# Attention scores of both mixers in steps of two heads of each key head, and no masked key tile for query tile 0

## What is computed

```python
# first mixer: window_attention, query blocks of 128, keys |i - j| <= 128 of 256, and 256 context keys
logits = concat([q . k (valid), q . k_ctx]) * HEAD_DIM ** -0.5
p = softmax(concat([logits, sink_of_head]))[..., :-1]
out = p @ concat([v, v_ctx])

# second mixer: nsa_attention, for each query block of 128
p_cmp = softmax(where(cmp_ok, q . k_cmp, NEG_INF)) * cmp_ok
p_slc = softmax(where(key_pos <= t_idx, q . k_sel, NEG_INF))
p_win = softmax(where(kpos <= t_idx, q . k_win, NEG_INF))
o = g0 * (p_cmp @ v_cmp) + g1 * (p_slc @ v_sel) + g2 * (p_win @ v_win)
```

## Time and profile before

| | us |
|---|---|
| median of 3 runs | 2797.01 |
| lowest and highest of them | 2795.85, 2802.97 |
| the profiled execution | 2805.34 |
| span in its profile | 2803.4 |
| PE busy | 2281.8 (81%) |
| DVE busy | 1179.1 (42%) |
| ACT busy | 497.4 (18%) |
| POOL busy | 1080.0 (39%) |

### The profile page before, as it was taken

One profiled execution on the slowest core, in us unless ns is written; L12 is line 12 of the kernel. 1 busy time (PEld: TensorE's weight loads), 2 busy tenths in 40 slices (PEclk: granted clock), 3 DMA queues, 4 the chain that ended last, 5 costly groups with the idle time before them and its releaser, 6 DMA issues.

```text
span 2803.4 us, 21791 instructions
## 1 busy us (share of the span) xinstructions
PE 2281.8 (81%) x7703; PEld 1058.7 (38%) x7703; DVE 1179.1 (42%) x2839; ACT 497.4 (18%) x1068; POOL 1080.0 (39%) x1028
## 2 busy tenths in 40 slices
PE   6998877787777776977788777779886789998997
PEld 2463832222222225722222222234454353443433
DVE  1241666665656445766656755420344230101001
ACT  2131121121112111211112111110133110000001
POOL 0000377777677660777777777700000000000000
PEclk9968999999999998999999999989856889999998
DMA  8424499999999992899999999944500079999996
GB/s 329 150 90 156 180 391 409 409 406 407 406 407 406 404 398 93 306 408 409 407 407 406 384 376 391 409 166 144 177 0 1 9 283 395 395 393 393 393 394 238
DMA packets 292277, 864.10 MB, mean 308 GB/s; under 512 B 19372, under 2 KB 26668, under 8 KB 291912
## 3 DMA queue, kind: packets, MB, share of 16 engines
q0 software_dynamic: 147456, 536.94, 48.7%
q1 hardware_dynamic: 144712, 325.74, 31.2%
HBM read 861.55 MB, written 1.05 MB: 308 GB/s over the span
## 4 chain that ended last, share of the span: by engine, by line
PE 37%; DMA 29%; POOL 17%; issue 7%; DVE 5%; ACT 4%; SPq 2%; POOLq 0%; DVEq 0%; ACTq 0%
PE bank L1604 18%; DMA ring<-in_up,arena 15%; DMA arena<-in_w_up 9%; POOL arena L631 8%; POOL ring L631 8%; PE bank L1809 5%; PE bank L2061 5%; DMA arena<-in_up,arena 4%; SPq L603 2%; PE bank L1646 2%; PE bank L1658 1%; PE bank L1659 1%; PE bank L2104 1%; PE bank L1713 1%; ACT h L653 1%
## 5 line engine op out<-in xcount | busy, mean ns | idle before, releaser
L1809 PE MATMUL bank<-arena 128*128 128x512 f32 x1024 | 516.9, 639 | 147.3 <-DMA arena<-in_up,arena 112.4
L1809 PE MATMUL bank<-ring,arena 128*128 128x512 f32 x976 | 496.2, 636 | 161.8 <-DMA ring<-in_up,arena 161.6
L1151 DVE SCALAR_TENSOR_TENSOR ring<-ring,h 128x1024 f32<-128x1024 f32 x256 | 313.1, 1225 | 324.8 <-DMA ring<-in_down,arena 324.4
L631 POOL DMA_INDIRECT arena<-in_down,arena x256 | 264.7, 1034 | 478.2 <-DVE arena L1135 400.8
L1151 DVE SCALAR_TENSOR_TENSOR arena<-arena,h 128x1024 f32<-128x1024 f32 x256 | 313.8, 1226 | 205.1 <-DMA arena<-in_down,arena 203.5
L1809 PEld LDWEIGHTS bank<-arena 128*128 128x128 f32 x1024 | 188.0, 198 | 473.6 <-DMA arena<-in_up,arena 260.1
L1809 PEld LDWEIGHTS bank<-ring,arena 128*128 128x128 f32 x976 | 173.3, 195 | 482.8 <-DMA ring<-in_up,arena 347.7
L782 ACT ACTIVATE arena<-const,arena 128x128 f32<-128x128 f32 x500 | 191.0, 398 | 811.8 <-PE bank L1809 806.8
L631 POOL DMA_INDIRECT arena<-in_up,arena x256 | 272.7, 1065 | 108.0 <-PE bank L1809 63.1
L631 POOL DMA_INDIRECT ring<-in_up,arena x256 | 276.3, 1079 | 83.0 <-issue 47.8
L631 POOL DMA_INDIRECT ring<-in_down,arena x256 | 266.2, 1040 | 78.6 <-issue 77.7
(11 more groups left out here) (385 smaller groups left out, 1917.5 us busy)
## 6 DMA issues: line engine op xcount, KB each, us to landing
ring<-in_w_gate SPq DMA_DIRECT2D x32, 2048.0 KB, 18.7
ring<-in_mod_w SPq DMA_DIRECT2D x24, 2048.0 KB, 18.9
ring<-in_w_up SPq DMA_DIRECT2D x16, 2048.0 KB, 19.0
arena<-in_w_up SPq DMA_DIRECT2D x16, 2048.0 KB, 19.9
ring<-in_w_down SPq DMA_DIRECT2D x16, 2048.0 KB, 14.1
arena<-in_w_down SPq DMA_DIRECT2D x16, 2048.0 KB, 18.8
ring<-in_w_in SPq DMA_DIRECT2D x9, 2048.0 KB, 8.0
ring<-in_peer_w_q SPq DMA_DIRECT2D x8, 2048.0 KB, 8.0
```

Of the source, the lines that this page charges most:

```text
L631: pool.indirect_dma_start(out=gslot(l, kind, g, k), out_offset=None, in_=a[kind], in_offset=bass.IndirectOffsetOnAxis(ap=idx_all[:, t, 16 ...
L1151: v.scalar_tensor_tensor(out=row, in0=row, scalar=1.0, in1=h[:, t], op0=ALU.mult, op1=ALU.mult, accum_out=act[:, t, 16 * hh + k:16 * hh + ...
L1809: ins = pe.matmul(bank[2 * t + c][:, :], diag[:, n % 4], row[:, 512 * c:512 * c + 512], start=hh == 0 and k == 0, stop=hh == 7 and k == up ...
```

## The change

A step now takes two query heads of each key head: step `it` has slots `p = 2 * (it % 2)` and the next one, and within the step the four products `n` go through key heads 0, 1, 0, 1. Products that follow each other therefore read opposite halves of the partitions. The number of products, their banks, their semaphores and their places in PE's queue stay as they are. DVE's readout is the same in the first mixer; its sink, its maximum and its output are addressed in the new order of heads. The values in each product are those of the head's own key head.

In the second mixer, tile 0 leaves out the second key tile: products of 256 columns instead of 512, readout of 2 x 128, maximum and gating over 8 x 128, exponentials of 128 columns. Tile 1 keeps its sizes.

```diff
--- before.py
+++ after.py
@@ -837,7 +837,7 @@
                 act_.activation(pcT[0:64], bank[6][0:64, :].rearrange("p (k t) -> p k t", k=4), ACT.Copy).then_inc(S["c_pt_ev"], 1)
                 for j in range(2):
                     it = 2 * t + j
-                    psc = pscs[j]
+                    psc = pscs[j][:, :, 0:P * (t + 1)]
                     act_.wait_ge(S["b_negm"], it + 1)
                     for q in range(8):
                         act_.activation(psc[:, q], psc[:, q], ACT.Exp, bias=nst[:, 1, q:q + 1],
@@ -1055,11 +1055,20 @@
             v.wait_ge(S["in_rows"], 16)
             win = cst("win").rearrange("p (t k) -> p t k", t=NT)
 
+            def by_pair(ap, it):
+
+                return ap.rearrange("p (j a) -> p a j", j=2)[:, 2 * (it % 2):2 * (it % 2) + 2]
+
+            def by_pair_out(ap):
+
+                return ap.rearrange("p (a j) -> p a j", j=2)
+
             def softmax1(it):
 
-                t, j = it // 2, it % 2
+                t = it // 2
                 sc1, ast = scs[it % 2], asts[it % 2]
-                sink = rw("sink")[:, 4 * j:4 * j + 4]
+                sink = by_pair(rw("sink"), it)
+                top, less = (by_pair_out(ast[:, i]) for i in (0, 3))
                 if it >= 2:
                     v.wait_ge(S["a_pt"], 4 * (it - 1))
                 for p in range(4):
@@ -1069,21 +1078,22 @@
                     v.tensor_scalar(sc1[:, p, 256:512], bank[p][:, 256:512], 0.125, None, ALU.mult).then_inc(S["a_s_ev"], 1)
                 v.wait_ge(S["a_s_ev"], 4 * it + 4)
                 link(v.tensor_reduce(ast[:, 0], sc1, AX, ALU.max))
-                link(v.tensor_tensor(ast[:, 0], ast[:, 0], sink, ALU.max))
-                v.tensor_tensor(ast[:, 3], sink, ast[:, 0], ALU.subtract)
+                link(v.tensor_tensor(top, top, sink, ALU.max))
+                v.tensor_tensor(less, sink, top, ALU.subtract)
                 v.tensor_scalar(ast[:, 2], ast[:, 0], -1.0, None, ALU.mult).then_inc(S["a_negm"], 1)
 
             def out1(it):
 
-                t, j = it // 2, it % 2
+                t = it // 2
                 ast = asts[it % 2]
                 v.wait_ge(S["a_exp"], 5 * it + 5)
                 link(v.tensor_tensor(ast[:, 4], ast[:, 4], ast[:, 3], ALU.add))
                 link(v.reciprocal(ast[:, 5], ast[:, 4]))
                 v.wait_ge(S["a_pv"], 4 * it + 4)
-                v.tensor_tensor(mixcat[:, t, 256 * j:256 * j + 256].rearrange("p (g d) -> p g d", g=4),
-                                bank[6 + it % 2][:, 0:256].rearrange("p (g d) -> p g d", g=4),
-                                bc(ast[:, 5], 2, 64), ALU.mult).then_inc(S["attn_o"], 1)
+                heads = mixcat[:, t, 0:512].rearrange("p (j a d) -> p a j d", j=2, a=4)
+                v.tensor_tensor(heads[:, 2 * (it % 2):2 * (it % 2) + 2],
+                                bank[6 + it % 2][:, 0:256].rearrange("p (a j d) -> p a j d", a=2, j=2),
+                                bc(by_pair_out(ast[:, 5]), 3, 64), ALU.mult).then_inc(S["attn_o"], 1)
 
             softmax1(0)
             for it in range(4):
@@ -1337,23 +1347,25 @@
                 v.tensor_tensor(p8, p8, bc(cmpok[:, t], 1, 8), ALU.mult).then_inc(S["c_p"], 1)
                 for j in range(2):
                     it = 2 * t + j
-                    psc = pscs[j]
+                    seen = P * (t + 1)
+                    psc = pscs[j][:, :, 0:seen]
                     if it >= 2:
                         v.wait_ge(S["b_pt"], 4 * (it - 1))
                     for p in range(4):
                         v.wait_ge(S["b_s"], 4 * it + p + 1)
-                        v.scalar_tensor_tensor(out=psc[:, 2 * p:2 * p + 2], in0=bank[p][:, :].rearrange("p (a k) -> p a k", a=2),
-                                               scalar=0.125, in1=bc(causal[:, t], 1, 2), op0=ALU.mult,
+                        v.scalar_tensor_tensor(out=psc[:, 2 * p:2 * p + 2],
+                                               in0=bank[p][:, 0:2 * seen].rearrange("p (a k) -> p a k", a=2),
+                                               scalar=0.125, in1=bc(causal[:, t, 0:seen], 1, 2), op0=ALU.mult,
                                                op1=ALU.add).then_inc(S["b_s_ev"], 1)
                     v.wait_ge(S["b_s_ev"], 4 * it + 4)
                     link(v.tensor_reduce(nst[:, 0], psc, AX, ALU.max))
                     v.tensor_scalar(nst[:, 1], nst[:, 0], -1.0, None, ALU.mult).then_inc(S["b_negm"], 1)
                     v.wait_ge(S["b_exp"], 8 * it + 8)
                     link(v.reciprocal(nst[:, 3], nst[:, 2]))
-                    gs = gsig[:, t, 12 * j:12 * j + 12].rearrange("p (a b) -> p a b", a=4)[:, :, 1:3]
-                    n3 = nst[:, 3].rearrange("p (a b) -> p a b", a=4)
+                    gs = gs3[:, 2 * j:2 * j + 2, :, 1:3]
+                    n3 = nst[:, 3].rearrange("p (a j b) -> p a j b", a=2, j=2)
                     link(v.tensor_tensor(n3, n3, gs, ALU.mult))
-                    v.tensor_tensor(psc, psc, bc(nst[:, 3], 2, T), ALU.mult).then_inc(S["b_p"], 1)
+                    v.tensor_tensor(psc, psc, bc(nst[:, 3], 2, seen), ALU.mult).then_inc(S["b_p"], 1)
 
             v.wait_ge(S["z_acts"], 1 + NT)
             for c in range(2):
@@ -1705,12 +1717,17 @@
                                     start=True, stop=True)
                 ins.then_inc(S["gmlp"], 1)
 
+            def head_of(it, n):
+
+                return 2 * (it % 2) + n // 2, n % 2
+
             def scores1(it):
-                t, j = it // 2, it % 2
-                for p in range(4):
+                t = it // 2
+                for n in range(4):
+                    p, j = head_of(it, n)
                     if it:
-                        pe.wait_ge(S["a_s_ev"], 4 * (it - 1) + p + 1)
-                    pe.matmul(bank[p][:, :], tile(qT[64 * j:64 * j + 64, p], t), kT[64 * j:64 * j + 64, :],
+                        pe.wait_ge(S["a_s_ev"], 4 * (it - 1) + n + 1)
+                    pe.matmul(bank[n][:, :], tile(qT[64 * j:64 * j + 64, p], t), kT[64 * j:64 * j + 64, :],
                               start=True, stop=True).then_inc(S["a_s"], 1)
 
             pe.wait_ge(S["operands_ev"], operand("tq1", 3))
@@ -1729,12 +1746,12 @@
                 ins.then_inc(S["a_pt"], 1)
 
             for it in range(4):
-                t, j = it // 2, it % 2
                 if it < 3:
                     scores1(it + 1)
                 turn1(4 * it)
                 for p in range(4):
                     k = 4 * it + p
+                    j = head_of(it, p)[1]
                     if p < 3:
                         turn1(k + 1)
                     pe.wait_ge(S["a_pt_ev"], k + 1)
@@ -1879,11 +1896,13 @@
             pe.transpose(bank[7][:, 0:64], kc2[0:64, 0:128], ident[0:64, 0:64]).then_inc(S["operands"], 1)
 
             def scores2(it):
-                t, j = it // 2, it % 2
-                for p in range(4):
+                t = it // 2
+                for n in range(4):
+                    p, j = head_of(it, n)
                     if it:
-                        pe.wait_ge(S["b_s_ev"], 4 * (it - 1) + p + 1)
-                    pe.matmul(bank[p][:, :], tile(nqT[64 * j:64 * j + 64, p], t), kswT[64 * j:64 * j + 64, :],
+                        pe.wait_ge(S["b_s_ev"], 4 * (it - 1) + n + 1)
+                    keys = kswT[64 * j:64 * j + 64, :].rearrange("p (a k) -> p a k", a=2)[:, :, 0:P * (t + 1)]
+                    pe.matmul(bank[n][:, 0:2 * P * (t + 1)], tile(nqT[64 * j:64 * j + 64, p], t), keys,
                               start=True, stop=True).then_inc(S["b_s"], 1)
 
             pe.wait_ge(S["operands_ev"], operand("tq2", 4))
@@ -1913,12 +1932,12 @@
                     ins.then_inc(S["b_pt"], 1)
 
                 for it in (2 * t, 2 * t + 1):
-                    j = it % 2
                     turn2(it, 0)
-                    for p in range(4):
-                        k = 4 * it + p
-                        if p < 3:
-                            turn2(it, p + 1)
+                    for n in range(4):
+                        k = 4 * it + n
+                        p, j = head_of(it, n)
+                        if n < 3:
+                            turn2(it, n + 1)
                         pe.wait_ge(S["b_pt_ev"], k + 1)
                         pe.wait_ge(S["c_pt_ev"], t + 1)
                         if t:
```

## The result

| | before | changed |
|---|---|---|
| median, us | 2797.7 (5 runs) | 2776.0 (5 runs) |
| lowest and highest | 2795.85, 2802.97 | 2765.66, 2779.43 |
| ratio of the runs | | 0.991, 95% interval 0.989 to 0.9931 |
| span of the profiled execution | 2803.4 | 2765.3 |

The changed kernel is faster by 25 us going by the ratio (19 to 31), 22 going by the medians. I had forecast 14.9 us, with 2773 us as the lower end of the range; 0.991 of 2797 is 2772, just beyond it; the changed kernel's own median, 2776.0, lies a little inside. Direction and places were right, the size was not. The profiled execution of the changed kernel took 2767.14 us, 8.9 under its median, and that of the kernel before some 8 over its own, so the two profiles lie 38 us apart where the medians lie 22.

The account below looks back on a forecast made before the run. Both attentions were taken as bound by their chain of waits, not transfers: PE's scores in the first mixer, mostly DVE and ACT in the second. 6.8 + 0.4 + 1.6 + 4.1 + 2.0 = 14.9 us off 2797.0 gives 2782.1; range 2773 to 2792.

Parts of the forecast that it names:

- four rounds and not five: Paired scores take four rounds of 0.85 us; rival, strict program order: five, saving 13.2 us, time 2783.8, chance 0.12.
- Step 0's maximum: First mixer: step 0's products are ready faster, DVE stops waiting between banks and the maximum starts earlier, saving 0.4 us.
- Tile 1 of the second mixer: First step: paired products finish 3.4 us earlier, DVE's readout becomes the bound, saving 1.6 us.
- Tile 0: Second mixer without the second key tile: shorter readout, maximum, exponentials and gating save 4.1 us in the first step, 2.0 in the second.
- the second step's readout and maximum: Second mixer, tile 0: hidden behind ACT's copies, so only exponentials and gating count there, 0.9 + 1.07 us.
- The second mixer as a whole: Saving of 7.7 us there: 1.6 from tile 1, 4.1 and 2.0 from the two steps of tile 0.
- Strides: New addressing costs -0.2 to +0.3 us, zero in the sum; rival, half-rate strided output in tile 0: 2785 us, chance 0.03.
- part 1: Alternate halves in both mixers: paired score products run side by side, saving 6.8 us, 0.4 and 1.6.
- 2 x 3.4 us: First mixer, scores of steps 2 and 3: 7.12 us become 3.7 at the lower clock, 6.8 us saved together.
- the clock among the rivals: Filled halves raise the granted clock for some 10 us, saving 5 us in one or both mixers: 2772 to 2777, chance 0.10.
- the direct part: First mixer: pairing halves the scores of steps 2 and 3 at the lower clock, worth 6.8 us.
- the slower rival: Products of 247.47 and 2113.75 lose the higher clock because PE is less busy before them: 2818 us, chance 0.03.

Follow-up runs that it names:

- its repetition: The changed kernel profiled again, no edit, in a later comparison with longer gathers: 2902.61 us, ratio 0.9919; first mixer 85.5 us.
- three with fillers: Changed kernel plus products that nobody reads where TensorE waits in the second mixer (2899.54 us; again 2883.87), or also two in the first mixer (2891.25).
- the short products: Kernel before, but products of steps 2 and 3 of the first mixer compute only the 256 window keys, in one half: 2793.73 us, ratio 0.9968.
- the long products in both halves: Kernel before, but products of steps 2 and 3 of the first mixer contract all 128 rows, summing two heads: 2787.46 us, ratio 0.9945.
- the kernel before with fillers: Kernel before plus products that nobody reads: in both mixers 2886.74 us, ratio 0.9837; two in the first mixer alone 2899.57 us, ratio 0.9905.
- the changed kernel with enough of them: Changed kernel plus products that nobody reads in both mixers, four instead of two in the first: 2890.09 us, ratio 0.989.

## Why the prediction fell short

**Where it was right.** The chain passes through the scores of steps 2 and 3, and what leaves it there leaves the whole: the gain at the start of the gathers was still there at the end. Pairs run fully side by side, in four rounds and not five: 3.71 us for eight passes at the lower clock is 0.3 and four times 0.85; five rounds would be 4.6. The Trainium skill ("TensorE: Matmul & The Clock Gate", Part 3, The mechanism) has products in different row groups start strictly in program order; the 3.71 us speak against that here. Step 0's maximum starts 0.5 us earlier, where I had 0.4 (157.15 and 157.63, of which 0.2 was there before the scores). Tile 1 of the second mixer: DVE's readout is the bound, as worked out. Tile 0: readout 1.34, maximum 1.23, exponentials 3.19 for eight, gating 1.24, where I had 1.35, 1.23, 3.2 and 1.23, and the second step's readout and maximum were hidden. The second mixer as a whole gave 7.3 for 7.7, and its shortening alone 6.3 for 6.1. Strides cost nothing that can be seen.

**The step that failed** is the one in part 1 that priced the first mixer at the lower clock throughout, 2 x 3.4 us, and put the clock among the rivals with one chance in ten and 5 us a mixer. The mechanism I named there was right and both of its numbers were too small. The rise was no accident: it came between 175.8 and 179.6 us in all six profiles in which step 2's scores began as pairs at the lower level (the changed kernel, its repetition, the alternation alone, three with fillers), and not in any of four profiles with products in one half and no fillers (the kernel before twice, the shorter tile alone, the short products), where the clock stayed at 0.50 from 163 to 166 us on until 204 or later. And it is worth more than 5 us, because PE's chain here is not only scores but transposes and value products that follow them for 30 us. By the runs: the direct part is 6.8 us (7.8 by the medians in the kernel of short products), and of the first mixer's 21.0 us 7.2 were mine; the remaining 14 are the clock, in line with the 13.8 us of the long products in both halves, which have no direct part. In the repetition the stage gave 16.9 us, which leaves the clock some 10: its worth moves with the moments at which it rises and falls.

What I read past: the row of step 2 showed 7.1 us of uninterrupted products at 0.50, while those of 2113.75, of 128 rows, had brought the clock up after 5.3 us, at 2119.0. I used that pair of rows against the slower rival and didn't ask what it says of scores that fill both halves.

**The two gains don't add as I took them to.** With the clock up, a pair saves half as much. Between the kernel before with fillers (81.7) and the changed kernel with enough of them (77.8) lie 3.9 us in the first mixer. My estimate for pairs at 2.4 GHz is as large: twice 1.7, half of the saving at the lower level, and 0.4 for step 0 make 3.8. It is one pair of profiles, and the two kernels differ in their number of fillers as well, so the agreement is no proof.

**What stays open.** What else than both halves it takes: from 164.0 to 172.5 us the kernel before had PE busy without a gap, with transposes and value products over all 128 rows, and the clock stayed at 0.50. Why the clock, once up, stayed for some 17 us in the changed kernel and 34 in the kernel with long products in both halves, I can't say from these runs. In the second mixer the alternation brought the clock up only briefly (from 2030 to 2037 us), and the fillers tried there brought it up only in parts; how to keep it up throughout isn't known.

## What to carry to other kernels

A change that fills more of TensorE's array has two prices, the passes it saves and the clock it may bring; where the chain runs through TensorE at 0.50 for tens of microseconds, work out the second one too, over everything that follows on the chain, and don't add it to the first at full size. Before taking trouble over such a change, try a few products that nobody reads in TensorE's nearest wait: here two of them, three lines, gave as much in the first mixer as the alternation. How many it takes has to be tried: with the alternation, two did nothing there and four took 3.6 us off. And where one profiled execution shows a clock rising at some point, look at a second one before it is built on.

## What was unexpected in the hardware

Eight passes of 64 rows and 512 columns in one half of the array ran 7.1 us without a gap, with other work of TensorE around them, and left the clock at 1.2 GHz in all three profiles in which they began there (the kernel before twice, the shorter tile alone); the same passes over all 128 rows raised it within their 5.73 us, and where fillers had kept it at 2.4 GHz it stayed there over them. Two streams in opposite halves don't wait for each other's place in program order, even with a semaphore wait and a signal on each product: 3.71 us for eight passes that take 7.12 in one half. And the same instructions ahead of the attention took 13.8 us in some executions and 17.1 to 17.8 in others, where the granted clock fell at another moment.
